# First norm of a hybrid encoder layer: low parts of two tiles and both weight splits ahead of the fourth tile's scaling

## The reference

```python
def rmsnorm(x, w):
    xf = x.astype(F32)
    y = xf * lax.rsqrt(jnp.mean(xf * xf, axis=-1, keepdims=True) + EPS)
    return (y * w.astype(F32)).astype(x.dtype)
...
def token_mixer(hn, w_in, lb, w_ret_norm, w_hg_norm, w_ret_up, w_hg_up, w_out):
    proj = hn @ w_in
...
        h = h + token_mixer(rmsnorm(h, norm_mix[l]), w_in[l], ...)
```

## Time and profile before

| | us |
|---|---|
| median of 3 runs | 1246.33 (1245.38 to 1246.88) |
| the profiled execution | 1245.58 |
| its span | 1243.8 |
| TensorE busy in it | 1210.3 (97%) |
| VectorE busy | 808.4 (65%) |
| ScalarE busy | 528.4 (42%) |
| GpSimd busy | 97.3 (8%) |

### The profile page before, as it was taken

One profiled execution on the slowest core, in us unless ns is written; L12 is line 12 of the kernel. 1 busy time (PEld: TensorE's weight loads), 2 busy tenths in 40 slices (PEclk: granted clock), 3 DMA queues, 4 the chain that ended last, 5 costly groups with the idle time before them and its releaser, 6 DMA issues.

```text
span 1243.8 us, 18442 instructions
## 1 busy us (share of the span) xinstructions
PE 1210.3 (97%) x6989; PEld 1100.5 (88%) x6989; DVE 808.4 (65%) x1217; ACT 528.4 (42%) x832; POOL 97.3 (8%) x109
## 2 busy tenths in 40 slices
PE   6999999999999999999999998999999999999986
PEld 5999899999999998888888888989989989989974
DVE  7594586378359454322323488797896897887787
ACT  5353335145145243222221247544545645536554
POOL 0000000000000000000000121112121111211120
PEclk9999999999999999999999999999999999999999
DMA  4301111211111111222124126555456465465552
GB/s 173 138 35 52 64 37 50 76 37 51 34 63 37 48 52 51 69 68 67 51 67 175 63 64 151 117 124 131 119 124 131 111 144 120 103 149 131 130 97 102
DMA packets 42192, 112.09 MB, mean 90 GB/s; under 512 B 4624, under 2 KB 4880, under 8 KB 42128
## 3 DMA queue, kind: packets, MB, share of 16 engines
q1 hardware_dynamic: 27584, 84.42, 19.8%
q0 software_dynamic: 13968, 25.43, 12.7%
q10 hardware_dynamic: 576, 1.38, 0.3%
HBM read 107.54 MB, written 3.15 MB: 89 GB/s over the span
## 4 chain that ended last, share of the span: by engine, by line
PE 89%; DVE 6%; ACT 1%; DVEq 1%; issue 1%; DMA 1%; SPq 0%; POOL 0%; ACTq 0%
PE ps L1586 45%; PE ps L1829 23%; PE ps L1912 10%; PE ps L1683 3%; PE ps L1623 3%; PE ps L1676 1%; DVE ring L1288 1%; PE ps L1693 1%; PE ps L1611 1%; DVE af L1309 1%; DVE h L1266 1%; PE ps L1613 1%; DMA raw<-in_pairs 0%; DVE gf L1394 0%; PE ps L1568 0%
## 5 line engine op out<-in xcount | busy, mean ns | idle before, releaser
L1586 PE MATMUL ps<-hn,ring 128*128 128x256 f32 (+1 forms) x2544 | 462.6, 337 | 0.3 <-DVE hn L966 0.3
L1586 PEld LDWEIGHTS ps<-hn,ring 128*128 128x128 f32 x2544 | 388.5, 191 | 46.7 <-issue 0.7
L1829 PE MATMUL ps<-af,ring 128*128 128x384 f32 x1848 | 325.3, 335 | 5.5 <-DVE af L1309 3.2
L1829 PEld LDWEIGHTS ps<-af,ring 128*128 128x128 f32 x1848 | 320.3, 188 | 9.7 <-DVE af L1309 4.8
L1912 PE MATMUL ps<-ring,gf 128*128 128x512 f32 x693 | 161.7, 391 | 6.9 <-DVE h L1266 3.9
L1912 PEld LDWEIGHTS ps<-ring,gf 128*128 128x128 f32 x693 | 129.2, 188 | 36.9 <-issue 6.0
L937 DVE TENSOR_TENSOR ring<-raw,ring 128x1024 fp32r<-128x1024 f32 x68 | 83.1, 1224 | 119.2 <-ACT ring L510 114.8
L753 ACT ACTIVATE ring<-raw 128x512 fp32r<-128x512 f32 x164 | 96.7, 622 | 48.8 <-DMA raw<-in_pairs 46.8
L1288 DVE TENSOR_TENSOR ring<-raw,ring 128x512 fp32r<-128x512 f32 x164 | 107.4, 684 | 13.5 <-ACT ring L753 13.2
L559 ACT ACTIVATE sig<-ps 128x768 f32<-128x768 f32 x36 | 29.2, 812 | 179.9 <-PE ps L1586 179.8
L510 ACT ACTIVATE ring<-raw 128x1024 fp32r<-128x1024 f32 x68 | 71.6, 1055 | 28.8 <-PE ps L1586 10.1
(11 more groups left out here) (172 smaller groups left out, 1215.8 us busy)
## 6 DMA issues: line engine op xcount, KB each, us to landing
raw<-in_units SPq DMA_DIRECT2D x68, 512.0 KB, 3.5
raw<-in_pairs SPq DMA_DIRECT2D x33, 512.0 KB, 4.3
raw<-in_pairs SPq DMA_DIRECT2D x66, 256.0 KB, 3.6
raw<-in_pairs POOLq DMA_DIRECT2D x64, 256.0 KB, 4.1
tb<-in_pairs POOLq DMA_DIRECT2D x31, 256.0 KB, 4.5
strips<-in_strips SPq DMA_DIRECT2D x4, 896.0 KB, 4.4
x_in<-in_x_s SPq DMA_DIRECT2D x4, 512.0 KB, 5.4
h<-in_x_s SPq DMA_DIRECT2D x1, 2048.0 KB, 8.1
```

What stands on the lines that cost most here:

```text
L1586: ins = pe.matmul(out, w if stationary_w else x, x if stationary_w else w, start=start and i == 0, stop=stop and i == 2)
L1829: ins = pe.matmul(ps[:, bank, 0:HALF], ring[:, p, a, k * P:(k + 1) * P], af[:, x, b, k, :], start=first and k == 0 and j == 0, stop=k == H ...
```

## The change

It reorders instructions on three engines; none is added or taken out. DVE's loop is written out: the low parts of the tiles 0 and 1 and both `split_lo` now stand ahead of tile 3's scale, and from tile 2 on `norm_low` of a tile stands directly behind that tile's own `weigh`. The wait for the norm's weights (`vec_ld`) moves from ahead of the first variance to ahead of the first `weigh`. On ACT the square of tile 4 moves ahead of `norm_hi` of tile 0, and that of tile 5 behind `split_hi` of unit 1. On TensorE only three tiles are transposed ahead of the first products; tile 3 is transposed behind (c, u) = (0, 0), tile 4 behind (0, 1), tile 5 behind (1, 0).

```diff
@@ ScalarE
-            for t in range(-3, NT):
-                if t + 3 < NT:
-                    act.wait_ge(x_ld[t + 3], 16)
-                    square(x_in[:, t + 3, :], t + 3, 0, junk[:])
-                if 0 <= t + 2 < NT:
-                    sqrt(t + 2, 0)
-                if t >= 0:
-                    norm_hi(t, 0, y32)
-                if t in (0, 1):
-                    split_hi(t, t)
+            def first_square(t):
+                act.wait_ge(x_ld[t], 16)
+                square(x_in[:, t, :], t, 0, junk[:])
+
+            first_square(0)
+            for t in range(3):
+                first_square(t + 1)
+                sqrt(t, 0)
+            first_square(4)
+            norm_hi(0, 0, y32)
+            sqrt(3, 0)
+            split_hi(0, 0)
+            norm_hi(1, 0, y32)
+            split_hi(1, 1)
+            first_square(5)
+            for t in range(2, NT):
+                norm_hi(t, 0, y32)
+                if t < 4:
                     sqrt(t + 2, 0)
@@ VectorE
+            def first_scale(t):
+                scale(x_in[:, t, :], t, 0, xn)
+
+            def first_weigh(t):
+                weigh(t, 0, V_MIX, 4 + 2 * (t % 2), y32)
+
+            variance(0, 0)
+            for t in range(2):
+                variance(t + 1, 0)
+                first_scale(t)
             dve.wait_ge(vec_ld, 32)
-
-            for t in range(-2, NT + 1):
-                if t + 2 < NT:
-                    variance(t + 2, 0)
-                if 0 <= t + 1 < NT:
-                    scale(x_in[:, t + 1, :], t + 1, 0, xn)
-                if 0 <= t < NT:
-                    weigh(t, 0, V_MIX, 4 + 2 * (t % 2), y32)
-                if t > 0:
-                    norm_low(t - 1, 0, y32)
-                if t in (1, 2):
-                    split_lo(t - 1, t - 1)
+            first_weigh(0)
+            variance(3, 0)
+            first_scale(2)
+            first_weigh(1)
+            norm_low(0, 0, y32)
+            split_lo(0, 0)
+            norm_low(1, 0, y32)
+            split_lo(1, 1)
+            first_scale(3)
+            first_weigh(2)
+            variance(4, 0)
+            norm_low(2, 0, y32)
+            variance(5, 0)
+            for t in (4, 5):
+                first_scale(t)
+                first_weigh(t - 1)
+                norm_low(t - 1, 0, y32)
+            first_weigh(5)
+            norm_low(5, 0, y32)
@@ TensorE
-            for t in range(4):
+            for t in range(3):
                 first_transposes(t)
...
-                        if c == 0:
-                            first_transposes(4 + u)
+                        if c == 0 or (c, u) == (1, 0):
+                            first_transposes(3 + 2 * c + u)
```

## The result

The changed kernel takes 1248.66 us (median of 22 runs, 1246.89 to 1250.25), the kernel before 1245.94 (22 runs, 1244.78 to 1249.01). The ratio is 1.0021, with a 95% interval of 1.0014 to 1.0027: slower by 2.6 us (the medians themselves lie 2.7 apart). The forecast was 1.2 us slower. The profiled executions stand at 1248.58 and 1245.58.

A forecast was written before the change was run, and what follows sets the result against it. TensorE's work plus its waits was taken as the bound (89% of the chain). Earlier products -2.10, tile 3's transposes +0.79, waits +1.02 and +1.49 sum to +1.20 us: 1246.33 + 1.2 = 1247.5 us, 8-in-10 range 1245.7 to 1249.3.

The forecast's parts named there:

- First products at 17.65: Start of TensorE's products: DVE's low part of tile 1 moves ahead, so they start 2.10 us sooner, at 17.65.
- DVE waits 1.14 us per tile for ACT: Norm loop: each low part right behind its own weigh makes DVE wait for ACT's high part, 1.14 us a tile.
- c = 1 at 27.95, c = 2 at 36.15: TensorE in the norm: waits for DVE's low parts, 1.02 us before c = 1 and 1.49 us before c = 2.
- c = 2 before the change at 34.95: TensorE in the kernel before: c = 2 begins with no wait at 28.24 + 0.79 + 2 x 2.96 = 34.95.
- Behind 29.27 nothing waits: From 29.27 on one block of TensorE's work, so microseconds won or lost earlier go one to one into the end.
- Behind the norm nothing is added: Unit 2: low parts come 3.03 us later, yet low part and free bank are in time by 1.3 and 0.4 us.
- The second rival: Behind the norm ACT is late for unit 2 and TensorE waits 0.6 us more: 1248.1 us; chance 0.08.
- net loss of 1.2 to 1.5 us: Whole kernel: the forecast's outcome, a net loss of this size, given a chance of 0.74.
- Can't be told from none: Whole time: a change under 0.2% (2.5 us) can't be told from none, and this one is 0.1%.
- slower by over 0.2%: Outcome class for the whole time, chance 0.11: the third rival and a twentieth of the rest.
- First and third rival: First: DVE's waits hidden, 1.31 us sooner, 1245.0 us, chance 0.10. Third: TensorE still slow through (0, 1), chance 0.08.
- The advance: Norm: the earlier start of the products, of which the first rival kept 2.10 - 0.79 = 1.31 us; chance 0.10.

The follow-up runs named there:

- e3: Changed kernel with the next tile's scale put between a tile's weigh and low part on DVE, roots of tiles 4 and 5 earlier on ACT: 1247.73 us.
- e4: Changed kernel with the next tile's scale or weigh between weigh and low part, and tile 5 transposed right behind tile 4: 1245.70 us.
- e1: Kernel before with two memsets on DVE ahead of tile 1's low part, a pure delay: 1248.73 us against 1246.29, ratio 1.0025.
- e2: Kernel before with four memsets on DVE ahead of tile 1's low part, a pure delay: 1250.01 us, ratio 1.0031.
- e7: Kernel before with 20 unused transposes of the identity in TensorE's wait of the last down product: 1244.97 us, ratio 0.9988.
- e8: Changed kernel with 20 unused transposes in TensorE's wait of the last down product: 1247.21 us, ratio 1.0008 to the kernel before.
- e9: Kernel before with TensorE's waits of the first norm filled nearly whole by unused transposes, plus 20 in the last down product: 1244.98 us.
- e10: Changed kernel with TensorE's waits of the first norm filled by unused transposes (8, 5, 28), plus 20 in the last down product: 1248.73 us.
- e5: Kernel before with 20 unused transposes of the identity (8, 2, 10) in TensorE's idle time of the first norm: 1247.20 us, ratio 1.0009.

## Why the prediction was right or wrong, point by point

- **First products at 17.65.** Measured 17.74; all of DVE's chain runs 0.09 late from the weigh of tile 0 on (10.70 for 10.61). ACT's square of tile 4 ran from 10.20 and ended 0.6 us before the high part was due, as worked out.
- **DVE waits 1.14 us per tile for ACT.** 1.06 to 1.13, four times. This is the step on which the forecast stood, and e3 and e4 show it: with a scale between weigh and low part the wait is 0.16 to 0.22 and the waits of TensorE shrink or go.
- **c = 1 at 27.95, c = 2 at 36.15.** Measured 27.99 and 36.22. The forecast counts the waits from start to start; so counted they were 0.54 us (27.99 less 26.66 + 0.79; 1.02 forecast, but the first products took 5.17 instead of 4.74, which the wait swallowed) and 1.51 us (36.22 less 31.75 + 2.96; 1.49 forecast).
- **c = 2 before the change at 34.95.** Too late by 0.14: I took 2.96 us for 24 products, a figure that holds the change-over to the transposes behind them; two runs of 24 in a row take 2.88 each. That, and 0.07 for c = 2, make the norm's cost 1.41 at c = 2 and, as measured at the landmark, 1.44 instead of 1.2.
- **"Behind 29.27 nothing waits", so that a gain or loss goes one to one into the end.** Rows 2 reach to 60 us, and only so far does it hold. In the profile of the kernel before TensorE waits 1.95 us before 1191.27 and 2.96 us before 1216.29, and in the changed kernel the clock fell behind the second of these waits, which is where the profiles' lag went from 1.6 to 3.0 us. In the medians of e1 and e2 a delay did pass nearly one to one (2.35 us at the landmark and 2.44 in the time; 3.61 and 3.72).
- **Behind the norm nothing is added, as far as unit 2.** Right: the sigmoid of unit 0 ended at 41.7 (41.55 forecast), TensorE had no wait between 36.22 and the landmark. The second rival didn't come.
- **The pace of TensorE.** Rows 7 read 1.00 at 23.2 us, where TensorE was still slow (4 products in that half microsecond, 6 in the one from 23.7); in the profile before there is simply no record of the granted clock ahead of 23.8 us, and the changed one shows 0.50 from 16.0 to 22.8. For the changed kernel the pace hardly mattered: I had summed it with the first products of the profile before, 4.74 us; they took 5.17, and the wait at c = 1 swallowed the 0.43. The 1.5 in the forecast's net loss of 1.2 to 1.5 us was my estimate for slower first products, and no run shows it; with 5.17 us for them the norm cost 1.44 at the landmark. What I missed is that the pace matters for the kernel before: I set a span that doesn't depend on the pace (41.02) against one execution of a span that does (36.1 to 38.3), and took that execution for the typical one.
- **The size, 1.2 for 2.6 us.** 1.44 is in the profiles. Of the rest, the comparison of e7 with e8 excludes the late falls (2.24 us apart without them). Its profile ties e8 down: no fall behind 25 us, 1247.04 for a median of 1247.21. The kernel before, with no fall behind 24 us in its profile, took 1245.58, while e7's median is 1244.97: typical executions of the order before are 0.6 us quicker than the one that I worked from. 1.44 + 0.6 + 0.17 = 2.2, and some 0.4 of the 2.6 stays open. That this 0.6 is the early pace is argued, not shown: the profiles of the order before without a fill at the norm have 4.58 (e7) and 4.74, and quicker ones weren't profiled. e7's own profile doesn't bear it out. It has the quicker first products and took 1245.86, 0.9 over e7's median, with a fall of the clock at 1184.0.
- **"Can't be told from none".** 2.6 us can, with 22 runs of each: the interval begins at 1.0014. At 1.0021 the change lies, just, in the class "slower by over 0.2%", which had 0.11 (0.08 and a twentieth of 0.92 make 0.13), and not in the one that had 0.86. The time is inside the range of 1245.7 to 1249.3, in part by luck: the 0.7 us of width was meant for longer hand-overs and the second rival, neither of which came, and was used up by what the forecast had left out.
- **First and third rival.** The advance did not survive. The third, at 0.08 and with that in the 0.11 for "slower by over 0.2%", was my estimate for a TensorE that is still slow through (0, 1), and no run shows it: in the changed kernel the clock was 1.00 from 22.8 on, and the 24 products of (0, 1) took 2.96 us (23.70 to 26.66).

## What to carry to other kernels

Where two engines hand a tile to and fro, put another tile's work between the two halves: a consumer that stands right behind its producer's input pays the other engine's whole duration, here 1.1 us a tile (0.16 to 0.22 with a scale between them, in e3), and an earlier start of 2.0 us did not make up for it here. When a pipelined loop is written out to move one step ahead, every later pair that the loop kept apart has to be looked at again. And where the first matmuls are on the path, one profile of a start-up is one draw (here the first 24 products took 4.58 to 5.26 us in five of the six profiles of the order before, and 2.95 in e9): what hides the slow start and what pays it are compared over several executions.

## What the runs showed of the hardware that was not expected

- The granted clock fell to 0.50 for 3.4 us behind late waits of 2 to 4 us (idle time from 1.94 in e7 to 3.55 in e9) in ten of the fourteen profiles, and not behind waits of the same length in others (the 2.96 us in the kernel before, 3.59 in e10). 20 transposes of 0.12 us in a wait of 3 us were worth 1.3 us in the median (e7), and no profile with this fill has a fall behind that wait.
- Half a fill did not help: in e5 TensorE came to 1.00 early (from 11.9 us), stood idle for 2.4 us, and was at 0.50 from 18.7 to 25.5, just when the products ran. In e9, with 1.1 us idle at most, it stayed at 1.00.
- The same load of 512 KB, with the same transfers around it in the program, took 4.0 (e1, e5) to 6.1 us (e10) to land.
